# Three entry stages by halves of the rows, four last tiles by rows, and a final normalisation in two passes

## What is computed

```python
h = h + jnp.concatenate([hm, ha], axis=-1) @ w_out[i]
h = h + (p[i] @ w_ple[i]) * jax.nn.sigmoid(h @ w_ple_gate[i])
return rmsnorm(h, norm_final)
```

```python
hin = x * (1.0 + mod[:, 1]) + mod[:, 0]
y = mla_mixer(hin, ...)          # or moba_mixer
x = layer_norm(DEEPNORM_ALPHA * x + mod[:, 2] * y, ln_g[i, 0], ln_b[i, 0])
hin = x * (1.0 + mod[:, 4]) + mod[:, 3]
y = conv_ffn(hin, ...)
x = layer_norm(DEEPNORM_ALPHA * x + mod[:, 5] * y, ln_g[i, 1], ln_b[i, 1])
```

## Time and profile before

| | before |
|---|---|
| median of 3 runs | 966.38 us (966.18 to 966.75) |
| the profiled execution | 967.04 us |
| its span, first to last instruction | 965.3 us |
| PE busy | 905.8 us, 94% |
| DVE busy | 683.0 us, 71% |
| ACT busy | 451.8 us, 47% |
| POOL busy | 102.3 us, 11% |
| share of PE in the chain that ended last | 87% |

### The profile page before, as it was taken

One profiled execution on the slowest core, in us unless ns is written; L12 is line 12 of the kernel. 1 busy time (PEld: TensorE's weight loads), 2 busy tenths in 40 slices (PEclk: granted clock), 3 DMA queues, 4 the chain that ended last, 5 costly groups with the idle time before them and its releaser, 6 DMA issues.

```text
span 965.3 us, 14566 instructions
## 1 busy us (share of the span) xinstructions
PE 905.8 (94%) x5804; PEld 772.6 (80%) x5804; DVE 683.0 (71%) x1068; ACT 451.8 (47%) x713; POOL 102.3 (11%) x69
## 2 busy tenths in 40 slices
PE   4999999999999899979999999879999799999993
PEld 4887878666776687769899998768997799999993
DVE  3487567575766766679987787876776798656455
ACT  4464444444444644445544444345554455445440
POOL 0000001000000210003111011221000042101004
PEclk9999999999999999989999999979999799999997
DMA  7966546345657473337997878818563279655501
GB/s 274 336 240 217 176 140 209 122 156 182 219 195 255 182 255 117 130 115 278 362 335 266 304 278 270 321 48 324 178 216 117 80 285 330 210 179 189 161 1 44
DMA packets 56188, 200.20 MB, mean 207 GB/s; under 512 B 6412, under 2 KB 7348, under 8 KB 56120
## 3 DMA queue, kind: packets, MB, share of 16 engines
q1 hardware_dynamic: 55816, 198.21, 59.4%
q0 software_dynamic: 304, 1.06, 0.4%
HBM read 198.18 MB, written 1.06 MB: 206 GB/s over the span
## 4 chain that ended last, share of the span: by engine, by line
PE 87%; DVE 7%; issue 2%; ACT 2%; POOL 1%; DMA 1%; POOLq 0%; SPq 0%; DVEq 0%
PE ps L985 25%; PE ps L986 24%; PE ps L987 24%; PE ps L1160 4%; PE ps L1061 2%; PE ps L1181 1%; PE ps L1167 1%; PE ps L998 1%; DVE arena L1272 1%; DVE wsp L1211 1%; PE ps L1121 1%; PE ps L1087 1%; DVE small L1654 1%; DMA X<-in_x 1%; PE ps L1149 1%
## 5 line engine op out<-in xcount | busy, mean ns | idle before, releaser
L985 PE MATMUL ps<-XT,wsp 128*128 128x256 f32 x768 | 220.6, 287 | 6.6 <-DVE wsp L1211 4.3
L986 PE MATMUL ps<-XT,wsp 128*128 128x256 f32 x768 | 216.5, 282 | 0.0
L987 PE MATMUL ps<-XT,wsp 128*128 128x256 f32 x768 | 216.2, 282 | 0.0
L1211 DVE TENSOR_TENSOR wsp<-ring,wsp 128x1024 fp32r<-128x1024 f32 x135 | 168.4, 1258 | 19.6 <-ACT wsp L1742 19.6
L1742 ACT CAST wsp<-ring 128x1024 fp32r<-128x1024 f32 x135 | 140.4, 1046 | 66.0 <-PE ps L987 62.8
L985 PEld LDWEIGHTS ps<-XT,wsp 128*128 128x128 f32 x768 | 146.4, 191 | 13.8 <-DVE wsp L1211 6.8
L986 PEld LDWEIGHTS ps<-XT,wsp 128*128 128x128 f32 x768 | 146.3, 190 | 1.1 <-issue 0.2
L987 PEld LDWEIGHTS ps<-XT,wsp 128*128 128x128 f32 x768 | 146.0, 190 | 0.0
L985 PE MATMUL ps<-wsp,ra 128*128 128x512 f32 x244 | 98.2, 403 | 4.5 <-POOL ra L2105 1.5
L1211 DVE TENSOR_TENSOR wsp<-arena,wsp 128x1024 fp32r<-128x1024 f32 x73 | 93.8, 1291 | 10.0 <-ACT wsp L1742 10.0
L1742 ACT CAST wsp<-arena 128x1024 fp32r<-128x1024 f32 x73 | 76.3, 1047 | 51.3 <-PE ps L987 51.3
(11 more groups left out here) (257 smaller groups left out, 1568.8 us busy)
## 6 DMA issues: line engine op xcount, KB each, us to landing
ring<-in_mod_w SPq DMA_DIRECT2D x68, 512.0 KB, 4.6
arena<-in_mod_w SPq DMA_DIRECT2D x28, 512.0 KB, 5.0
ring<-in_ffn_a SPq DMA_DIRECT2D x25, 512.0 KB, 4.6
ring<-in_ffn_b SPq DMA_DIRECT2D x24, 512.0 KB, 4.7
arena<-in_ffn_o SPq DMA_DIRECT2D x23, 512.0 KB, 4.7
ring<-in_ffn_o SPq DMA_DIRECT2D x21, 512.0 KB, 4.7
arena<-in_ffn_b SPq DMA_DIRECT2D x20, 512.0 KB, 5.1
arena<-in_ffn_a SPq DMA_DIRECT2D x19, 512.0 KB, 4.6
```

What stands on the lines that cost most here:

```text
L985: pe.matmul(o, l[0], r[0], start=start, stop=False)
L986: pe.matmul(o, l[0], r[1], start=False, stop=False)
L987: return pe.matmul(o, l[1], r[0], start=False, stop=stop)
L1211: ve.tensor_tensor(w[:, 1024:1024 + n], raw[slot[0]][:, 0:n], w[:, 0:n].bitcast(f32), SUB).then_inc(*done("V", "lo", u, also=[("raw", *slo ...
```

## The change

`transposed_rows` is new: it does the transposes and the high and low parts of one half t alone, with two transposes into each of four banks, and operations of 2 x 128 columns in place of 512. The gate, `mla_c` and `moba_v` are entered with it for t = 0. Their first column block (`between` given) takes all its four tiles together: four for t = 0, then the transposes and parts for t = 1, then four for t = 1. `tail` now takes the last four tiles by rows and not the last two. The feed-forward layers take the last four tiles (rounds 9 and 10) by rows, and the second half in the order of the column blocks. The residual's addition is on DVE throughout. The final normalisation is made in two passes of DVE: (x - mean) * g, then times the inverse deviation plus b, for each quarter of the output, in place of a normalisation and two operations shared by DVE, ACT and POOL.

```diff
+    def proj_a(x, nk, name, base, blocks, evac, tail=False, before=None, between=None):
...
-                m = 2 if tail and cb == blocks - 1 and q == nq - 2 else 1
+                m = 4 if tail and cb == blocks - 1 and q == nq - 4 or between and cb == 0 else 1
...
-                if m == 2:
+                if m == 4:
                     W.still = True
                 got = [W.next(name, base + cb * nq + q + e) for e in range(m)]
                 for t in range(2):
-                    add("row", x, nk, got, q, t, bs[t], prior("bank", bs[t]), q + m == nq)
+                    if t and between and cb == 0:
+                        between()
+                    for e in range(m):
+                        add("row", x, nk, [got[e]], q + e, t, bs[t], prior("bank", bs[t]), q + e + 1 == nq)
+                        if t:
+                            W.done(got[e][1], 0.5 if m == 4 else 1.0)
+                        elif m == 4:
+                            W.step(0.5)
                     if q + m == nq:
                         evac(t, cb, bs[t])
                         bank.put(bs[t][0])
                 q += m
-                for u, p in got:
-                    W.done(p)
...
+    def transposed_rows(tag, nk, kind, t):
+        banks, pending = {}, []
...
+        for k in range(0, nk, 2):
+            b = banks[k] = bank.get()
+            add("trr", tag, k, t, b, prior("bank", b))
+        for k in range(0, nk, 2):
+            b = banks[k]
+            if kind is None:
+                add("xr_hl", tag, k, t, b)
+            else:
+                s = wk.get()
+                add("xr_m", tag, k, t, b, s, prior("wk", s))
+                pending.append((k, s))
+                if len(pending) > 1:
+                    low_part()
+            bank.put(b[0])
...
+        if t:
+            W.still = False
...
-    transposed("x1", 8, None, apart=True)
+    transposed_rows("x1", 8, None, 0)
...
-    proj_a("x1", 8, "w_gate", 0, 2, ev_gate, True)
-    add("rms2_x", 1)
+            add("rms2_x", t)
+    proj_a("x1", 8, "w_gate", 0, 2, ev_gate, True, between=lambda: transposed_rows("x1", 8, None, 1))
...
+    def finals(t):
+        for cb in range(2):
+            add("out_g", t, cb, final[0])
+        for cb in range(2):
+            add("out", t, cb, final[1])
...
+        def ends():
+            W.still = True
+            gs = [held.pop(0), held.pop(0)]
+            got = [W.next(f"ffn_o{i}", 18 + j) for j in range(4)]
+            for t, j, cb in [(0, j, cb) for j in range(4) for cb in range(2)] + \
+                    [(1, j, cb) for cb in range(2) for j in range(4)]:
+                o = outs[t][cb]
+                add("fo", i, 9 + j // 2, t, j % 2, cb, got[j], gs[j // 2], o, prior("bank", o), j == 3, t == 1)
+                if j == 3:
+                    resid(1, i, t, cb, o)
+                    bank.put(o[0])
+                if t and cb:
+                    W.done(got[j][1])
...
-    proj_a("m00", 8, "mla_c", 0, 1, ev_cq)
+    proj_a("m00", 8, "mla_c", 0, 1, ev_cq, between=lambda: transposed_rows("m00", 8, "m", 1))
...
+                    ve.scalar_tensor_tensor(x, x, mv2[:, t * 4:t * 4 + 1], raw[g[0]][:, cs], SUB, MUL).then_inc(
+                        *done("V", "out_g", t, cb))
...
+                    ve.scalar_tensor_tensor(x, x, mv2[:, t * 4 + 2:t * 4 + 3], raw[g[0]][:, cs], MUL, ADD).then_inc(
+                        *done("V", "out", t, cb))
```

More of the change, by code:

```diff
@@ L586, in modulated @@
         until(i, 1 if which == 0 else 4)
-        transposed(f"m{i}{which}", 8, "m", apart=True)
+        if which:
+            transposed(f"m{i}1", 8, "m", apart=True)
+        else:
+            transposed_rows(f"m{i}0", 8, "m", 0)
     def gain(tag, name, off, bias):
@@ L633, in ffn, with second @@
         held, hold = [], {}
-        def second(u, ends):
+        def second(u):
             g = held.pop(0)
[L637 to L640, removed]
+            for e in range(2):
+                w = W.next(f"ffn_o{i}", 2 * u + e)
+                for t in range(2):
                     for cb in range(2):
                         o = outs[t][cb]
[L643 to L656, removed]
-            gp.put(g[0])
+                        add("fo", i, u, t, e, cb, w, g, o, prior("bank", o), False, t == 1 and cb == 1)
+                W.done(w[1])
+            gp.put(g[0])
+        def ends():
[11 more added lines that the diff above has]
+                    W.done(got[j][1])
+            for g in gs:
+                gp.put(g[0])
         for u in range(11):
@@ L676, in ffn @@
             proj_b(f"m{i}1", 8, f"ffn_b{i}", 2 * u, 2, evb)
-            if u:
-                second(u - 1, False)
-        second(10, True)
+            if 0 < u < 10:
+                second(u - 1)
+        ends()
     modulated(0, 0)
@@ L1000, in tensor @@
                                 ins.then_inc(*done("P", "tr", tag, k))
+                elif kind == "trr":
+                    tag, k, t, b, before = a
+                    for i in range(2):
+                        src, event = source(tag, t, k + i)
+                        for e in new("P", event, before, ("cst",)):
+                            pe.wait_ge(*e)
+                        ins = pe.transpose(ps[b[0]][:, i * 128:(i + 1) * 128], src, ID)
+                    ins.then_inc(*done("P", "tr", tag, k, t))
                 elif kind == "blk2":
@@ L1031, in tensor @@
                             kg = 2 * (q + e_) + k
-                            for e in new("P", ("lo", u), ready(x, kg), before):
+                            for e in new("P", ("lo", u), ready(x, kg, t), before):
                                 pe.wait_ge(*e)
@@ L2069, in pool @@
                     x = {"g0": "m00", "g1": "m01", "g2": "m10", "g3": "m11"}[tag]
[L2070 removed]
+                    for e in new("G", xr(x, 1), ("gain_a", tag, n), ("gain", tag, n, 0),
                                  ("gain", tag, n - 1, 1) if n else None):
```

155 lines of the change are left out of this document (88 added, 67 removed).

## The result

| | before | changed |
|---|---|---|
| median | 966.57 us (966.18 to 967.64, 4 runs) | 1010.08 us (1009.61 to 1012.15, 4 runs) |
| the profiled execution | 967.04 us | 1012.15 us |
| its span | 965.3 us | 1010.4 us |
| PE busy | 905.8 us | 917.3 us |

The ratio is 1.045 (95% interval 1.0437 to 1.0462): slower by 43.5 us. The forecast was 1001, with a range of 984 to 1013. The profiled executions differ by 45.1 us.

What follows compares the result with a forecast made beforehand. PE was taken to bound the kernel, with time to win or lose only where stages meet. Terms 22.4 + 6.1 + 6.1 + 2.9 - 2.8 = +34.7 on 967.04 gave 1001.7, less 0.66, 1001 us; range 984 to 1013.

Steps and rivals of the forecast that it cites:

- the likeliest case: All stages: casts and low parts queue behind the work ending t = 1; +34.7 us, to 1001; chance 0.5.
- the rival "clock": Every new gap restarts PE at 1.2 GHz; seven uncounted gaps at about 1.5 us give 1010; chance 0.2.
- feed-forward 0, entry, and the later low part: Low parts follow XT's last one, +4.9 us; a modulation step ahead of a later low part, +1.2.
- ffn_lo: End of feed-forward 0: by rows PE has 2.8 us of covering work, not 5.6, while POOL finishes; +2.4 us.
- MoBA, entry: Into MoBA: DVE's residual addition ends the norm earlier, first matmul at E+7.3 (E: last matmul's end) against 10.9; -3.6 us.
- MoBA: tiles, turn, second block: Inside MoBA: tiles two to four wait for low parts +1.3, t = 0 to t = 1 +2.3, second block's first tile +2.
- I take two more such restarts, about +2: The clock's share of the point forecast, 2 us, which the milder rival would leave out.
- -1.5: MoBA: less of the work falls under the low clock; -1.5 us.
- Compression, entry: Into MLA's compression: ACT does XT's two scalings and four copies before the first cast; +2.05 us over 7.65.
- Modulation ahead of `moba_o`'s fourth tile: Ahead of feed-forward 1: that tile's low part stands behind six residual operations and one modulation step; +1.3 us.
- Edits at nothing: Additions taken from POOL, last blocks of `w_out` and `mla_o` by rows, and loads: priced at no cost.
- Halves pay: Rival: casts and low parts do not delay PE, entries gain, waits for weight tiles under 2 us; 965 us; chance 0.05.

Runs made afterwards that it cites:

- pre3: The changed kernel with casts and low parts of the next tiles listed as each of the first three tiles is done for t = 1, everywhere: 988.69 us.
- inner: The changed kernel with next tiles' casts and low parts listed ahead only inside the blocks entered by halves, not where a residual stage ends: 996.50 us.
- fill: The changed kernel with idle transposes of the identity on PE in ten of its gaps, sized to some 90% of each: 997.35 us.
- halves: The changed kernel with two last tiles by rows, as before, in place of four; the three entries by halves and the small edits stay: 995.81 us.
- ordered: The kernel of best with only the compression entered by halves, the gate's last four tiles by rows, and the list reordered for it: 971.06 us.
- best: The kernel before with the two-pass end, last four tiles by rows and additions on DVE, in the last feed-forward layer alone: 963.57 us.
- best_fill: The kernel of best with idle transposes of the identity on PE inside 13 waits at its five entries: 956.43 us.

## Why the prediction was right, point by point

The mechanism was the likeliest case's: low parts behind the work that ends t = 1. The time was that of the rival "clock", 1010. Both are borne out, the first by pre3 and inner (21 and 13.6 us back by order alone, some 9 and 5 of them in PE's busy time and so by the clock), the second by fill (12.7 us with the gaps as they were). Without the clock, the terms were forecast at 34.2 us and measured at 32.5, with errors of both signs; the clock was forecast at +0.5 and measured at +11.5, and that is nearly all that the point forecast of 1001 lacked. That the rival "clock" met 1010 is in part luck: it took seven more restarts at 1.5 us or less, where five came, of 1.6 to 3.1 us each.

| step of the prediction | forecast | measured |
|---|---|---|
| into the gate | +1.1 | +1.16 |
| gate, t = 0 to t = 1 | +3.75 | +3.78 |
| gate, first to second block | +5.3 | +5.24 |
| into the compression | +2.05 | +2.90 |
| compression, t = 0 to t = 1 | +4.2 | +4.53 |
| compression to the next projection | +4.0 | +4.11 |
| feed-forward 0, entry, and the later low part | +4.9, +1.2 | +4.36, +1.4 |
| feed-forward 1, entry, and `moba_o` | +4.8, +1.3 | +4.35, 0 |
| `ffn_lo` | +2.4 | +1.62 |
| MoBA, entry | -3.6 | -3.10 |
| MoBA: tiles, turn, second block | +1.3, +2.3, +2 | +0.88, +2.48, +2.26 |
| end | -2.8 | -3.5 |
| clock, all stages | +2 and -1.5 | +11.5 |

The terms measured come to 44.0; 1.1 of the 45.1 us are left. The transposes of X, 14.0 us busy before and 12.2 now, stand in the gaps and in PE's busy time both; counted once, the clock's term is 13.3, and the terms come to 45.8, 0.7 too many. The prediction's "five of these six gaps" is a miscount: two of the six are entries at which PE waited before (2.7 and 7.65 us), and four are new.

- **The step that was mis-sized** is "I take two more such restarts, about +2" together with MoBA's "-1.5". The clock did not fall anew in two gaps but in five: the gate's turn to t = 1 and its second block, the compression's turn, the gap ahead of MLA's keys, and MoBA's second block. Each cost some 1.6 to 3.1 us behind it (half of PE's busy time at the low clock). The reason given against the rival, that the gate's entry had kept its clock, was true and did not carry over: that entry keeps it in the changed kernel too (2.83 us idle), and so do the wait for `ffn_lo` (3.16), MoBA's turn (1.44) and the later low part in feed-forward 0 (1.40). Nor did MoBA save its share, since its first matmuls came earlier and so took the low clock that the transposes had taken before. The Trainium skill ("TensorE: Matmul & The Clock Gate", HAM oscillation) describes a loop in which each idle wait ends in a restart at half clock. The trace agrees at five of nine new or longer waits at places that were at full clock before, and not at the other four.
- **Compression, entry.** 0.85 us over. The chain to the scaled X of t = 1 is as forecast (E+4.5), but the parts of XT take ACT to E+8.3 and not to 7.5. The prediction counted two scalings and four copies; ACT has four scalings and four copies there, back to back at 0.385 us, as each block of 128 columns is scaled by an instruction of its own (L1857).
- **Modulation ahead of `moba_o`'s fourth tile** cost nothing; no such wait is in the trace.
- **`ffn_lo`.** POOL's operation took 2.72 us in place of 3.85, between the 3.85 and 1.55 us that the prediction put beside each other. The wait is the 2.8 us of cover that went, less 1.1 of a quicker POOL.
- **Edits at nothing.** In the changed kernel I saw no cost of the norm's new place, as t = 0 ends 5.6 us ahead there and its norm is through before t = 1 ends. With two last tiles by rows the same edit costs 5.4 us, which I had not foreseen, and the additions on DVE cost 0.9 at MoBA's entry.
- **Halves pay.** Their gains at the entries came almost as this rival had them (1.35, 1.75 and 2.1 us in halves, against its 1.2, 1.6 and 1.6), but the waits for weight tiles were far over its 2 us. So they do not pay as written, and not in the one other order that was tried for the compression (ordered). That another order of the gate's and MLA's lists could pay is open.

## What to carry to other kernels

When tiles are held longer so that one half can go ahead, look at what makes the next tiles: a part that is free earlier is worth nothing if its cast stands in an in-order queue behind the work that ends the held block, and putting it ahead helps only where that work is short. Price a wait of PE with the clock that may fall behind it: here the new gaps cost some 33 us and the low clock another 11.5, and idle transposes in known waits took 0.7% off a kernel that was already tuned (best to best_fill). Taking the last tiles by rows paid in the one place where it was tried alone, at the very end (3.4 us with the two-pass end, best), where nothing has to be ready next.

## What was not expected of the hardware

- How long PE idled did not alone decide whether the clock fell. Behind 1.8 us (pre3, between the gate's blocks) it read 0.58 from 312 to 316, and behind 3.16 us (`ffn_lo` in the changed kernel) it read 1.00 from 657 to 660. Nor did the same wait always end alike: behind the gate's entry, 3.86 us in the changed kernel and 3.87 in inner, it read 1.00 from 288 to 292 in the one and 0.50 from 290 to 292 in the other. So which waits cost a restart is read off one execution here, and the count of five can differ in another.
- Restarts were dearer than taken. Behind the gate's gap 12 matmuls of 512 columns took 0.43 us each in place of 0.23, which is 2.4 us.
- Idle transposes of one identity, 0.11 us each, are enough to hold the clock at 1.00 through feed-forward 0's entry of 8.3 us (best_fill, 418 to 438 us).
